# The first three tiles behind two RMS norms multiplied ahead of the root, and their banks scaled afterwards

## The reference

```
def rms_norm(x, g):
    y = x32 * lax.rsqrt(jnp.mean(x32 * x32, axis=-1, keepdims=True) + EPS)
    return (y * g)
...
h = rms_norm(x, norm1_g[l])
proj = h @ w_in[l]                      # q, k, v, z, xbc, dt, two gates
q = rms_norm(q.reshape(B_, S_, N_HEADS, HEAD_DIM), q_norm_g[l])
k = rms_norm(k.reshape(B_, S_, N_HEADS, HEAD_DIM), k_norm_g[l])
...                                     # attention, SSD mixer, gates
x = x + mixed @ w_out[l]
x = x + peer_ffn(rms_norm(x, norm2_g[l]), w_peer_q[l], ...)   # queries, keys, top 16, 16384 experts
```

## Time and profile before

| | |
|---|---|
| median of 3 runs | 2103.1 us (2100.53 to 2109.51) |
| profiled execution | 2104.44 us, its span 2102.7 us |
| PE busy | 98% of the span |
| DVE, ACT, POOL busy | 74%, 53%, 13% |
| mean granted TensorE clock | 0.992 of full speed |

### The profile page before, as it was taken

The page is one execution under the profiler, slowest core; times in us unless marked ns, Lnnn a source line. Parts: engine busy times, 40 slices in busy tenths (PEclk is TensorE's granted clock), DMA queues, the critical chain, the costliest instruction groups (busy, mean ns, idle before and its releaser), DMA issues.

```text
span 2102.7 us, 40254 instructions
## 1 busy us (share of the span) xinstructions
PE 2056.2 (98%) x16766; PEld 1998.7 (95%) x16766; DVE 1555.5 (74%) x2733; ACT 1120.2 (53%) x1743; POOL 277.3 (13%) x265
## 2 busy tenths in 40 slices
PE   7999999999999999999999999999999999999998
PEld 7898998999999999999999999998899999999998
DVE  6777789775899777887777668656567887877764
ACT  5557678644544566654444445465345554445553
POOL 0000000000888444430000000000110000000000
PEclk9999999999999999999999999999999999999999
DMA  5433433566555444445766767433115677654553
GB/s 195 167 133 127 137 125 114 198 234 230 181 186 186 143 143 143 144 142 211 251 240 231 273 240 250 167 131 110 56 41 187 246 251 259 216 195 171 184 181 121
DMA packets 104437, 375.43 MB, mean 179 GB/s; under 512 B 11584, under 2 KB 12224, under 8 KB 103872
## 3 DMA queue, kind: packets, MB, share of 16 engines
q1 hardware_dynamic: 104256, 372.86, 51.0%
HBM read 370.71 MB, written 2.10 MB: 177 GB/s over the span
## 4 chain that ended last, share of the span: by engine, by line
PE 75%; DVE 17%; ACT 4%; issue 2%; DMA 2%; POOL 0%; SPq 0%; POOLq 0%; DVEq 0%; ACTq 0%
PE ps L374 21%; PE ps L376 20%; PE ps L375 20%; PE ps L777 3%; DVE wl L1557 3%; DVE arenap L1899 2%; ACT wh L1104 1%; DVE arena L1700 1%; PE ps L571 1%; DMA raw<-in_ada 1%; PE ps L460 1%; DVE arenap L1864 1%; PE ps L461 1%; PE ps L462 1%; DVE arenap L1859 1%
## 5 line engine op out<-in xcount | busy, mean ns | idle before, releaser
L374 PE MATMUL ps<-xah,wh 128*128 128x256 f32 x2800 | 798.2, 285 | 7.2 <-DVE wl L1557 3.0
L375 PE MATMUL ps<-xal,wh 128*128 128x256 f32 x2800 | 787.4, 281 | 0.0
L376 PE MATMUL ps<-xah,wl 128*128 128x256 f32 x2800 | 787.2, 281 | 0.0
L1104 ACT ACTIVATE wh<-raw 128x1024 fp32r<-128x1024 f32 (+1 forms) x608 | 620.5, 1036 | 277.3 <-PE ps L376 133.4
L1557 DVE TENSOR_TENSOR wl<-raw,wh 128x1024 fp32r<-128x1024 f32 (+2 forms) x539 | 637.7, 1204 | 167.0 <-ACT wh L1104 165.8
L374 PEld LDWEIGHTS ps<-xah,wh 128*128 128x128 f32 x2800 | 528.6, 189 | 19.9 <-issue 9.8
L375 PEld LDWEIGHTS ps<-xal,wh 128*128 128x128 f32 x2800 | 528.6, 189 | 0.5 <-issue 0.2
L376 PEld LDWEIGHTS ps<-xah,wl 128*128 128x128 f32 x2800 | 528.4, 189 | 0.0
L2271 POOL TENSOR_TENSOR wl<-raw,wh 128x1024 fp32r<-128x1024 f32 (+1 forms) x69 | 162.7, 2364 | 1181.9 <-ACT wh L1104 1181.7
L374 PE MATMUL ps<-hh,wh 128*128 128x256 f32 x1024 | 289.9, 283 | 6.4 <-DVE wl L1557 4.7
L375 PE MATMUL ps<-arenar,wh 128*128 128x256 f32 x1024 | 287.7, 281 | 0.0
(11 more groups left out here) (354 smaller groups left out, 3057.7 us busy)
## 6 DMA issues: line engine op xcount, KB each, us to landing
raw<-in_pu SPq DMA_DIRECT2D x128, 512.0 KB, 3.3
raw<-in_pv SPq DMA_DIRECT2D x128, 512.0 KB, 3.5
raw<-in_ada SPq DMA_DIRECT2D x96, 512.0 KB, 4.2
raw<-in_ff_up SPq DMA_DIRECT2D x88, 512.0 KB, 3.4
raw<-in_w_xbc SPq DMA_DIRECT2D x32, 512.0 KB, 3.2
raw<-in_ff_down SPq DMA_DIRECT2D x32, 512.0 KB, 4.0
raw<-in_w_z SPq DMA_DIRECT2D x16, 512.0 KB, 3.2
raw<-in_w_so SPq DMA_DIRECT2D x16, 512.0 KB, 4.3
```

The lines of the kernel that those rows point to most:

```text
L374: mm(o, w0, x0, start=start, stop=False, skip_group_check=skip)
L375: mm(o, w0, x1, start=False, stop=False, skip_group_check=skip)
L376: return mm(o, w1, x0, start=False, stop=stop, skip_group_check=skip)
L1104: put(W.hi(i), W.raw(i), ACT.Copy).then_inc(S["high"], 1)
```

## The change

Before the root is known, ACT makes `x1h` = x * gain (high part, L1151 of the changed kernel) and DVE `x1l` (L1653), for all 8 slices of each of the two norms. Tiles 0, 1 and 2 of `qk` and of `pq` are multiplied from these. DVE copies the root's row to SBUF (`rows1`) and multiplies each of the six banks with it when its tile is done (`scaled_bank`, L1658), into `hrw` or `pq`; ACT's copies of these banks go. The slice-by-slice tiles and the filler go for these two norms. The mean and the row are issued between units. In `qk` the first two `head_stat` stand after tile 2 instead of after tiles 0/1 and 2. The conversions of the weights are written at other places among the norm's steps. J and cst are loaded behind the first two weight units.

```diff
+            tile(("qk", 0), "w_q", 0, 8, X1, unscaled(0), range(6))
+            t.wait_ge(S["ld_J"], 16)
+            t.wait_ge(S["ld_cst"], 16)
+            mean("n1", J1024, sq1)
+            tile(("qk", 1), "w_q", 2, 8, X1, unscaled(0), range(6), root_row("n1"))
+            tile(("qk", 2), "w_q", 4, 8, X1, unscaled(0), range(6))
+            head_stat(0)
+            head_stat(1)
+            for i in range(3, 8):
+                tile(("qk", i), ("w_q", "w_k")[i // 4], 2 * (i % 4), 8, XA, n1, range(6))
+                head_stat(i - 1)
             head_stat(7)
...
+            tile(("pq", 0), "w_pq", 0, 8, X1, unscaled(1), HIGH, root_mean())
+            row("n2")
+            tile(("pq", 1), "w_pq", 2, 8, X1, unscaled(1), HIGH)
+            next(mo, None)
+            next(mo, None)
+            tile(("pq", 2), "w_pq", 4, 8, X1, unscaled(1), HIGH, mo)
+            for i in range(3, 8):
+                tile(("pq", i), "w_pq", 2 * i, 8, XA, n2, HIGH, mo)
...
+            def unscaled(k, g):
+                put(x1h[:, k], xT[:, k, :], ACT.Copy, scale=pc(g, k)).then_inc(S["x1_hi"], 1)
...
             for k in range(8):
+                if k == 4:
+                    halves(1)
+                unscaled(k, "norm1")
+            for k in range(8):
                 square("n1", k, xT, sq1)
+                if k in (3, 7):
+                    halves(k // 4 + 2)
+            a.wait_ge(*B.is_full(("n1", "stat")))
             root("n1")
+            halves(W.at[("qk", 2), 1, 0] + 1)
             for k in range(8):
+                if k == 4:
+                    halves(W.at[("qk", 3), 0, 0] + 1)
                 plain("n1", k, hbuf, XA)
...
-                residual("n2", i, ("out", i), xT, sqo)
+                residual("n2", i, ("out", i), xT, sqo, lambda k: unscaled(k, "norm2"))
...
+            def norm_beside(name, x, g, buf, dst, beside):
+
                 for k in range(8):
                     scaled(name, k, x, g(k), buf)
+                    if k == 1:
+                        copy(rows1, B[(name, "row")][:, 0:256]).then_inc(S["rows1"], 1)
                     if k:
                         plain_lo(name, k - 1, buf, dst)
+                    if k in beside:
+                        beside[k]()
                 plain_lo(name, 7, buf, dst)
+
+            def unscaled_lo(n, k, g):
+                v.wait_ge(S["x1_hi"], 8 * n + k + 1)
+                stt(x1l[:, k], xT[:, k, :], pc(g, k), x1h[:, k].bitcast(f32), ALU.mult, ALU.subtract).then_inc(S["x1_lo"], 1)
+
+            def scaled_bank(n, key, dst):
+                v.wait_ge(S["rows1"], n + 1)
+                v.wait_ge(*B.is_full(key))
+                tt_(dst.rearrange("p (a b) -> p a b", b=256), pair(B[key]), rows1.unsqueeze(1).to_broadcast([128, 2, 256]),
+                    ALU.mult).then_inc(B.empty(key), 1)
...
+                if i == 1:
+                    v.wait_ge(S["hn"], 1)
+                    scaled_bank(0, ("qk", 2), hrw[:, 0, :])
```

More of the change, by code:

```diff
@@ L179, in build @@
             xbh, xbl = sb(part, "xbh", [128, 16, 256], f32r), sb(part, "xbl", [128, 16, 256], f32r)
+            with ExitStack() as over:
+                sb(over, "before_x1", [128, 74 * 256])
+                x1h, x1l = sb(over, "x1h", [128, 8, 256], f32r), sb(over, "x1l", [128, 8, 256], f32r)
             ar1 = sb(part, "arena1", [128, 99 * 256])
@@ L592, in head_stat, with root_row @@
                 mm(P[:, :], B64, hs2[:, i % 2, :], start=True, stop=True).then_inc(B.full(("hs", i), len(W.units)), 1)
[L593 to L599, removed]
+            def root_row(name, ids=range(8)):
+                row(name, ids)
+                yield
+            tile(("qk", 0), "w_q", 0, 8, X1, unscaled(0), range(6))
[9 more added lines that the diff above has]
+                head_stat(i - 1)
             head_stat(7)
@@ L728, in pe, with root_mean @@
             W.mark("spill")
-            stat("n2", J1024, sqo)
             def n2(k):
                 t.wait_ge(*step_of("n2", "x", k))
[L734 to L740, removed]
+            def root_mean():
+                mean("n2", J1024, sqo)
+                yield
+            tile(("pq", 0), "w_pq", 0, 8, X1, unscaled(1), HIGH, root_mean())
[6 more added lines that the diff above has]
+                tile(("pq", i), "w_pq", 2 * i, 8, XA, n2, HIGH, mo)
             run(mo)
@@ L1113, in square, with residual, slice_in @@
                 put(sq[:, k, :], x[:, k, :], ACT.Square).then_inc(S["norm_sq"], 1)
-            def residual(name, i, key, x, sq):
+            def residual(name, i, key, x, sq, ahead=None):
+                def slice_in(k):
+                    if ahead:
+                        ahead(k)
+                    square(name, k, x, sq)
                 if i == 3 and (key, 0) in B.units:
@@ L1162, in act @@
                 P = bank(("qk", i))
[L1163 to L1164 removed]
+                if i > 2:
+                    a.wait_ge(S["hn"], i - 1)
+                    put(hrw[:, i % 2, :], P[:, :], ACT.Copy).then_inc(B.empty(("qk", i)), 1)
                 a.wait_ge(*B.is_empty(("qk", i)))
@@ L1667, in dve @@
             v.wait_ge(S["ld_pc"], 16)
+            v.wait_ge(S["ld_x"], 16)
+            for k in range(8):
+                if k == 4:
+                    lows(1)
+                unscaled_lo(0, k, "norm1")
+            lows(2)
+            sums("n1", sq1, 2)
+            lows(3)
+            sums("n1", sq1, 3)
+            rms("n1")
+            norm_beside("n1", xT, lambda k: pc("norm1", k), hbuf, XA, {
+                0: lambda: lows(W.at[("qk", 2), 1, 0]), 2: lambda: scaled_bank(0, ("qk", 0), hrw[:, 0, :]),
+                3: lambda: lows(W.at[("qk", 2), 1, 0] + 1), 5: lambda: scaled_bank(0, ("qk", 1), hrw[:, 1, :]),
+                6: lambda: lows(W.at[("qk", 3), 0, 0] + 1)})
+            v.wait_ge(S["g8"], 1)
             v.wait_ge(S["ld_cst"], 16)
-            for i in (2, 3):
-                sums("n1", sq1, i)
-            norm("n1", xT, lambda k: pc("norm1", k), hbuf, XA)
-            v.wait_ge(S["g8"], 1)
             def head(i):
```

42 lines of the change are left out of this document (28 added, 14 removed).

## The result

The changed kernel takes 2115.83 us (median of 7 runs, 2113.29 to 2119.13), the kernel before 2103.10 (7 runs, 2097.97 to 2109.51). The ratio is 1.0059, 95% interval 1.0047 to 1.0071. The same kernel measured again beside others came to 1.0075 (1.0061 to 1.0088). The change costs 12 to 16 us, 0.6 to 0.75%. Both medians are of whole executions; what follows on single places is read from one profiled execution of each kernel.

A forecast was written before the change was run, and what follows sets the result against it. PE, busy 98%, was taken as the bound, with DVE as good as a second bound from 33 to 82 us. Terms 6.4 + 4.1 + 2.1 = +12.6 on the median 2103.1 gave 2115.7, forecast as 2116; range 2104 to 2122.

The forecast's parts named there:

- First norm, +6.4 forecast: First norm: head 0 and `wl` 7 come late on DVE, so PE is 6.4 us late from the v weights on.
- The wait of about 2 us for ACT's copy: First norm: a PE idle of about 2 us, ended by ACT's copy near 51.
- the single bank: First norm: tile 4 needs tile 3's bank, whose copy waits for head 1; unit 8 starts at 52.0, 6.5 late.
- The drop of the clock at unit 7: First norm: the low clock behind PE's 4.6 us wait is hidden by head 1.
- Second norm, +4.1 forecast: Second norm: PE waits 4.9 us at the chunk sum for DVE's list and is 4.1 late.
- DVE's list of 13.4 us behind the row: Second norm: DVE's work from the row to the modulation's second pair, 13.6 us, ending at 492.2.
- Slice 7's low part: Second norm: `x1l` of slice 7 ready at 472.5, with PE waiting for slices 6 and 7 until then.
- The clock, +2.1 forecast: Second norm: low clock costs up to 1.7 behind the chunk sum's wait, 0.4 at slices 6 and 7; bounds 0 and 4.
- B: Both norms: the same two waits, but shorter and at full clock; +8.7, 2112 us; chance 0.22.
- C: Both norms: not slower, PE's head start stays; 2096 us, 2103 if half holds; chance 0.11 with its halves.
- the right two points: First norm: `wl` 7 before 41.5; second norm: the last modulation pair (L1653) before 483.5; trace against both by over 4 us.
- D: Second norm: unit 137's weights, behind the spill of x, land after 480; up to +5 on top, 2121; chance 0.10.

The follow-up runs named there:

- e3: Changed kernel with unit 7's low parts made ahead of head 0's reciprocal on DVE; 2116.56 us, ratio 1.0056.
- e10: Changed kernel with products nobody reads filling two PE waits, ahead of unit 7's and the second norm's chunk sum; 2116.68 us, ratio 1.0059.
- e5: e3 with, besides, a bank of its own for each of tiles 3 to 7 in place of one shared; 2115.03 us, ratio 1.0066.
- e9: e5 with parts of units 3 and 4 made while waiting for the mean, and the row inside unit 2; 2114.90 us, ratio 1.0053.
- e8: e7 with unit 1 asked for only behind slice 6 of unit 0, and the modulation's pair back ahead of the low parts; 2102.66 us, ratio 1.0002.
- e11: Changed kernel with both norms mended, the first as in e9, the second as in e8; 2102.44 us, ratio 0.9998.
- e7: Changed kernel with the first norm as before the change, second norm's tile 0, adds, row and chunk sum rearranged; 2107.66 us, ratio 1.0024.
- e4: Changed kernel with the second norm's chunk sum one unit later on PE alone; 2111.27 us, ratio 1.0034.

## Why the prediction was right, and where only its sum was

2116 was forecast and 2115.8 measured, slower by more than 0.5% as the likeliest. The steps behind it were not all as good as their sum.

**First norm, +6.4 forecast, 5.5 measured.** Each step is in the trace, early by about one microsecond. `pcol` landed 0.5 earlier (0.6). PE began at 12.31 (12.1). I had the whole of unit 0 at the low clock, and its products rise to full speed at 15.7, within the unit, so the mean ended at 21.1 (22.0), the root at 23.3 (24.3), the row at 25.4 (26.6), head 0 began at 38.6 (40.1). Unit 7 waited 4.3 (4.6), unit 8 began at 50.8 (52.0). The wait of about 2 us for ACT's copy, which I had said would show, is not there: unit 7 at the low clock ran into its place. e3 and e10 bring it out, 4.25 and 1.91 us, so the single bank was a bound behind the `wl`, as the step said. The drop of the clock at unit 7 cost next to nothing, as the step said too: e10, without it, starts unit 8 at 50.2 for 50.8. That the first norm is DVE's matter is shown by e5 and e9: take away the `wl`'s place and the bank, and what is left follows the begin of head 0.

**Second norm, +4.1 forecast.** The mechanism held: DVE's list of 13.4 us behind the row (13.6) makes the chunk sum wait 5.06 (4.9). One step I missed, and by itself it cost nothing: tile 0 waits 1.7 us for a bank. It may take only banks 4 to 7, and the next one, bank 4, was the modulation's, which DVE frees behind two pairs L1705. I had read bank use for q and k and not here; but slice 7 would have held the tile anyway. Whether the clock would have fallen without this wait no run shows by itself. Slice 7's low part was ready at 478.8, less the 5.7 carried 473.1 (472.5), and that is the 0.6 by which this term was too small.

**The clock, +2.1 forecast.** This is the term that was mis-sized. I had 0.4 for the waits at slices 6 and 7 and 1.7 behind the chunk sum. But 1.7 and 1.9 us of wait with seven slices' products between them brought the low level for 480 to 486, and it fell on unit 1 of tile 0, which took 5.3 us (480.99 to 486.25) for 2.9, ahead of the row on which DVE's whole list hangs: 2.4. Behind the sum, 500 to 506 are at 0.55, and between the sum and the keys PE loses another 3.1 (12.6 late at 500.75, 15.7 at the keys). Together 5.5 for 2.1. The Trainium skill, "TensorE: Matmul & The Clock Gate", section "Why this matters for your kernels", warns of idle gaps between bursts of matmuls; the trace agrees for the wait of 5.1 us, and shows the low level behind the two shorter ones as well. So from 444 to the keys the loss is 10.0, where 4.1 and 2.1 were forecast; 0.6 of slice 7 and 3.4 of clock make up the difference to within 0.2.

**The sum.** 6.4 + 6.2 = 12.6 stood against 15.7 at the keys, and 13.0 at the end. That the total fits is partly luck: the execution before that was profiled spent 3.3 us more between 1594 and 1805 than the one after, in code that the change doesn't touch and with some 10 us at the low clock there for some 7, and the second measurement (1.0075) lies at the 15.7.

**The rivals.** B (full clock) is out by the rows at 0.50. C named the right two points: `wl` 7 before 41.5, which e3 does at 38.2, and the modulation's pair in time, which e8 and e11 reach in effect by moving the sum. But its prices were wrong. At the first norm the point was not enough, since the bank and then DVE's heads bounded PE, and e9 is still 1.7 us late. At the second e8 wins 1.3 us of 4.6. So C's "not slower" can be had, and no order that I ran comes near its 2096. D (late weights) is in the trace as a wait of ACT, 2.80 us for a unit of w_pq until 484.2, which is 478.5 less what was carried, before D's 480: it was hidden behind the row at 486. In e7 0.23 us of it reach PE.

## What to carry to other kernels

Work that frees the first engine to start early is paid by the engine that makes its operands; here PE gained 7 us of head start and DVE got 10 us of work in stretches in which it was already the second bound, and the best order of it that I ran only breaks even. When a wait is mended and the time doesn't move, look in the trace for the same microseconds one unit later: three bounds stood behind each other here (a low part, one shared bank, the heads). And a group of instructions whose place is free, like the chunk sum, is worth moving first: one unit later was worth 5.8 us up to the keys, and some 5 us in the median (2111.3 for 2115.8 and 2116.7).

## What the runs showed of the hardware

A wait of 2.93 us of PE was followed by 3.5 us at a granted clock of 0.52 (e7), waits of 4.3 and 5.1 likewise, and two of 1.7 and 1.9 with the products of seven slices between them too; in e8 waits of 0.7 to 1.0, and in e4 one of 2.21, left it at 1.00. A wait of 1.80 was followed by 0.62 over 4 us in e10, while the same wait of 1.70 in the kernel before was not. So the length of one wait alone doesn't tell these cases apart. Filler of 128x128 products, 4.18 us for 36, kept the clock up through a wait.

The column of the granted clock doesn't tell everything at the very start. In the changed kernel it says 1.00 from 12 us on, but the products stand 0.21 us apart until 15.7 and 0.12 after that, where the same form at 44.6 and a clock of 0.50 stands 0.21 apart too:

```profile
12.00:14.00 2.00, 1.69 (x8) 1.69 (x9) 1.84 (x5) 2.00 (x7) 0.00 (x0) 1.00 1.03 412
14.00:16.00 2.00, 2.00 (x11) 2.00 (x11) 1.20 (x2) 2.00 (x6) 0.00 (x0) 1.00 0.84 332
16.00:20.00 4.00, 4.00 (x37) 4.00 (x35) 2.88 (x5) 0.95 (x1) 0.00 (x0) 1.00 0.42 134
```

At the start of a trace, read the level from the spacing of equal products.
